# A two-layer encoder on one core: stationary weight tiles read with a step of two values, weight slots at six places modulo 512 bytes

## What is computed

```python
x = x + 0.5 * swiglu(rmsnorm(x, norm_ff1[i]), ff1_w_gate[i], ff1_w_up[i], ff1_w_down[i])   # d_ff = 2816
x = x + token_mixer(rmsnorm(x, norm_mix[i]), w_in[i], ...)      # sparse attention + gated linear attention
x = x + 0.5 * swiglu(rmsnorm(x, norm_ff2[i]), ff2_w_gate[i], ff2_w_up[i], ff2_w_down[i])
g = jax.nn.sigmoid(rmsnorm(x, norm_ple[i]) @ ple_w_gate[i])
x = x + g * (p[i] @ ple_w_proj[i])
```

## Time and profile before

| what | value |
|---|---|
| runs | 1181.10 and 1181.36 us, median 1181.23 us |
| span of the profiled execution, first to last instruction | 1179.5 us |
| PE busy | 1168.9 us (99%), 10534 matmuls |
| PEld busy | 1144.7 us (97%) |
| DVE busy | 814.0 us (69%) |
| ACT busy | 593.7 us (50%) |
| granted TensorE clock, mean | 0.997 of full speed |
| moved by DMA | 218.87 MB, mean 186 GB/s |

### The profile page before, as it was taken

One profiled execution on the slowest core, in us unless ns is written; L12 is line 12 of the kernel. 1 busy time (PEld: TensorE's weight loads), 2 busy tenths in 40 slices (PEclk: granted clock), 3 DMA queues, 4 the chain that ended last, 5 costly groups with the idle time before them and its releaser, 6 DMA issues.

```text
span 1179.5 us, 24037 instructions
## 1 busy us (share of the span) xinstructions
PE 1168.9 (99%) x10534; PEld 1144.7 (97%) x10534; DVE 814.0 (69%) x939; ACT 593.7 (50%) x669; POOL 122.8 (10%) x136
## 2 busy tenths in 40 slices
PE   9999999999999999999999999999999999999997
PEld 9999999999999999999999999999899999999996
DVE  5866555688978766655786665558798777666455
ACT  5544445555745544444554444447367455444443
POOL 2000001011512000001210000100133020000011
PEclk9999999999999999999999999999999999999998
DMA  7655555545445555555555555554635365555541
GB/s 288 235 203 188 193 201 177 184 156 202 145 149 207 190 188 206 183 204 187 179 202 194 194 199 184 197 203 139 214 140 169 118 235 203 184 204 186 186 172 36
DMA packets 33384, 218.87 MB, mean 186 GB/s; under 512 B 5184, under 2 KB 6016, under 8 KB 7296
## 3 DMA queue, kind: packets, MB, share of 16 engines
q1 hardware_dynamic: 33280, 217.34, 53.2%
HBM read 216.15 MB, written 1.05 MB: 184 GB/s over the span
## 4 chain that ended last, share of the span: by engine, by line
PE 98%; DVE 1%; DMA 1%; ACT 0%; issue 0%; POOL 0%; SPq 0%; POOLq 0%; DVEq 0%
PE psum L385 31%; PE psum L387 31%; PE psum L386 31%; PE psum L665 1%; PE psum L644 1%; DMA x_all<-in_x 1%; PE psum L517 0%; PE psum L578 0%; PE psum L628 0%; PE psum L699 0%; PE psum L424 0%; PE psum L710 0%; PE psum L613 0%; DVE gates L1671 0%; PE psum L733 0%
## 5 line engine op out<-in xcount | busy, mean ns | idle before, releaser
L1222 DVE TENSOR_TENSOR w_lo<-raw,w_hi 128x2048 fp32r<-128x2048 f32 x200 | 457.9, 2293 | 213.5 <-ACT w_hi L856 213.4
L856 ACT ACTIVATE w_hi<-raw 128x2048 fp32r<-128x2048 f32 x201 | 385.2, 1917 | 366.6 <-PE psum L387 360.8
L385 PE MATMUL psum<-hA_hi,w_hi 128*128 128x256 f32 x1360 | 377.9, 278 | 0.0
L386 PE MATMUL psum<-hA_hi,w_lo 128*128 128x256 f32 x1360 | 375.7, 276 | 0.0
L387 PE MATMUL psum<-hA_lo,w_hi 128*128 128x256 f32 x1360 | 375.7, 276 | 0.0
L385 PEld LDWEIGHTS psum<-hA_hi,w_hi 128*128 128x128 f32 x1360 | 255.4, 188 | 2.7 <-issue 2.7
L386 PEld LDWEIGHTS psum<-hA_hi,w_lo 128*128 128x128 f32 x1360 | 255.4, 188 | 0.0
L387 PEld LDWEIGHTS psum<-hA_lo,w_hi 128*128 128x128 f32 x1360 | 255.3, 188 | 0.0
L385 PE MATMUL psum<-hB_hi,w_hi 128*128 128x256 f32 x832 | 230.3, 277 | 1.1 <-DVE w_lo L1654 1.1
L386 PE MATMUL psum<-hB_hi,w_lo 128*128 128x256 f32 x832 | 229.7, 276 | 0.0
L387 PE MATMUL psum<-hB_lo,w_hi 128*128 128x256 f32 x832 | 229.7, 276 | 0.0
(11 more groups left out here) (182 smaller groups left out, 1226.0 us busy)
## 6 DMA issues: line engine op xcount, KB each, us to landing
raw<-in_weights SPq DMA_DIRECT2D x203, 1024.0 KB, 4.9
raw<-in_weights SPq DMA_DIRECT2D x2, 512.0 KB, 6.2
out<-gates SPq DMA_DIRECT2D x3, 256.0 KB, 2.2
x_all<-in_x SPq DMA_DIRECT2D x1, 520.0 KB, 3.9
x_all<-in_x SPq DMA_DIRECT2D x1, 512.0 KB, 6.2
relu<-in_p SPq DMA_DIRECT2D x2, 256.0 KB, 5.0
consts<-in_consts SPq DMA_DIRECT2D x1, 384.0 KB, 5.7
out<-gates SPq DMA_DIRECT2D x2, 128.0 KB, 2.3
```

The costliest lines, as they stand in the source:

```text
L385: pe.matmul(o, lh, rh, start=start, stop=False)
L386: pe.matmul(o, ll, rh, start=False, stop=False)
L856: act.activation(w_hi[:, s, :], raw[:, s, :], ACT.Copy).then_inc(hi_ready[s], 1)
L1222: dve.tensor_tensor(w_lo[:, s, :], raw[:, s, :], w_hi[:, s, :].bitcast(F32), ALU.subtract).then_inc(lo_ready[s], 1)
```

## The change

The host alternates the columns of the two output tiles in each block of 256 (`in_turn` in `weight_chunks`, for the chunks of 8 x 256 columns): column 2j is column j of the first tile, 2j + 1 that of the second. The kernel reads a tile back with a step of two values (`in_turn(s)`, then `wh[:, k, c, :]`), so that the 128 values of a stationary tile lie over 1024 bytes where they lay over 512. Chunks of the other kinds are as before.

`w_hi` and `w_lo` become three tiles each, with gaps of 128 bytes: modulo 512, and from the same origin, `w_hi` is at 0, 128 and 256 and `w_lo` at 64, 192 and 320. `hA` and `small` stay at 192. The six small tiles move into the gaps; they leave the place ahead of `hB` and `hid`, and as `BEFORE_HB` is not changed, `hB` and `hid` come to 320. No instruction is added or taken away, on any engine, and no wait.

```diff
-LO_PLACE = 128
+LO_PLACE = 64
+SLOT_STEP = 128
...
-        w_hi = sb("w_hi", [P, SLOTS, 2048], F32R)
-        sb("before_w_lo", [P, LO_PLACE // 4])
-        w_lo = sb("w_lo", [P, SLOTS, 2048], F32R)
-        sb("before_hA", [P, (MOVING_PLACE - LO_PLACE) % 512 // 4])
+        w_hi, w_lo, between = [], [], []
+        for s in range(SLOTS):
+            w_hi.append(sb(f"w_hi{s}", [P, 2048], F32R))
+            between += [sb(f"between{s}{i}", [P, SLOT_STEP // 8]) for i in range(2)]
+        mean, rstd, r_eighth, r_less, r_half, gbias = (t[:, 0:2] for t in between)
+        sb("before_w_lo", [P, (LO_PLACE - SLOTS * SLOT_STEP) % 512 // 4])
+        for s in range(SLOTS):
+            w_lo.append(sb(f"w_lo{s}", [P, 2048], F32R))
+            sb(f"after_w_lo{s}", [P, SLOT_STEP // 4])
+        sb("before_hA", [P, (MOVING_PLACE - LO_PLACE - SLOTS * SLOT_STEP) % 512 // 4])
...
+            def in_turn(s):
+
+                return [w[s][:, :].rearrange("p (k i c) -> p k c i", k=8, c=2) for w in (w_hi, w_lo)]
+
             def by_columns(s, o, h, columns=(0, 1)):
-                wh, wl = (w[:, s, :].rearrange("p (k n) -> p k n", n=256) for w in (w_hi, w_lo))
+                wh, wl = in_turn(s)
                 for c in columns:
                     for k in range(8):
-                        mm = three(o[:, c * T:(c + 1) * T], wh[:, k, c * P:(c + 1) * P], wl[:, k, c * P:(c + 1) * P],
+                        mm = three(o[:, c * T:(c + 1) * T], wh[:, k, c, :], wl[:, k, c, :],
                                    h[0][:, k, :], h[1][:, k, :], k == 0, k == 7)
...
-                            mm = three(bank[DOWN_BANKS[m] + i][:, 0:T], wh[:, u, i * P:(i + 1) * P], wl[:, u, i * P:(i + 1) * P],
+                            mm = three(bank[DOWN_BANKS[m] + i][:, 0:T], wh[:, u, i, :], wl[:, u, i, :],
                                        hid[0][:, k, :], hid[1][:, k, :], k == 0, k == 21)
...
-                act.activation(w_hi[:, s, :], raw[:, s, :], ACT.Copy).then_inc(hi_ready[s], 1)
+                act.activation(w_hi[s][:, :], raw[:, s, :], ACT.Copy).then_inc(hi_ready[s], 1)
...
-                dve.tensor_tensor(w_lo[:, s, :], raw[:, s, :], w_hi[:, s, :].bitcast(F32), ALU.subtract).then_inc(lo_ready[s], 1)
+                dve.tensor_tensor(w_lo[s][:, :], raw[:, s, :], w_hi[s][:, :].bitcast(F32), ALU.subtract).then_inc(lo_ready[s], 1)
...
+    def in_turn(tiles):
+        return tiles.reshape(*tiles.shape[:-1], 2, P).swapaxes(-1, -2).reshape(tiles.shape)
+
+    def pairs(m, c0):
+        return in_turn(columns(m, c0, 256))
```

More of the change, by code:

```diff
@@ L397, in pairs @@
             def pairs(s, first, h, c, ks):
-                wh, wl = (w[:, s, :].rearrange("p (k n) -> p k n", n=256) for w in (w_hi, w_lo))
+                wh, wl = in_turn(s)
                 for k in ks:
-                    mm = three(bank[first + c][:, 0:T], wh[:, k, c * P:(c + 1) * P], wl[:, k, c * P:(c + 1) * P],
+                    mm = three(bank[first + c][:, 0:T], wh[:, k, c, :], wl[:, k, c, :],
                                h[0][:, k, :], h[1][:, k, :], k == 0, k == 7)
@@ L409, in by_tokens @@
             def by_tokens(s, o, h, ks, first, last, ahead=None):
-                wh, wl = (w[:, s, :].rearrange("p (k n) -> p k n", n=512) for w in (w_hi, w_lo))
+                wh, wl = (w[s][:, :].rearrange("p (k n) -> p k n", n=512) for w in (w_hi, w_lo))
                 for i, k in enumerate(ks):
@@ L480, in ffn @@
                     s = operands(L, off + DOWN + c)
-                    wh, wl = (w[:, s, :].rearrange("p (u n) -> p u n", n=256) for w in (w_hi, w_lo))
+                    wh, wl = in_turn(s)
                     for u in range(8):
@@ L534, in mix @@
                 wait_free(pe, L, "small")
-                wh, wl = (w[:, s, 0:1024].rearrange("p (k n) -> p k n", n=P) for w in (w_hi, w_lo))
+                wh, wl = (w[s][:, 0:1024].rearrange("p (k n) -> p k n", n=P) for w in (w_hi, w_lo))
                 for k in range(8):
@@ L797, in embed @@
                 pe.wait_ge(p_lo, L + 1)
-                wh, wl = (w[:, s, :].rearrange("p (k n) -> p k n", n=1024) for w in (w_hi, w_lo))
+                wh, wl = (w[s][:, :].rearrange("p (k n) -> p k n", n=1024) for w in (w_hi, w_lo))
                 for m in range(8):
@@ L886, in split_pieces @@
                 for i in range(4):
-                    act.activation(w_hi[:, s, piece(i)], raw[:, s, piece(i)], ACT.Copy).then_inc(piece_hi if i < 3 else hi_ready[s], 1)
+                    act.activation(w_hi[s][:, piece(i)], raw[:, s, piece(i)], ACT.Copy).then_inc(piece_hi if i < 3 else hi_ready[s], 1)
             def take_rb(L, k, b):
@@ L1112, in _ @@
                 for m in (2 * i, 2 * i + 1):
-                    act.activation(w_hi[:, 0, piece(m)], raw[:, 0, piece(m)], ACT.Copy).then_inc(piece_hi if m < 3 else hi_ready[0], 1)
+                    act.activation(w_hi[0][:, piece(m)], raw[:, 0, piece(m)], ACT.Copy).then_inc(piece_hi if m < 3 else hi_ready[0], 1)
             squares(0, 0, 0)
@@ L1116, in _ @@
             for i in range(4):
-                act.activation(w_hi[:, 1, piece(i)], raw[:, 1, piece(i)], ACT.Copy).then_inc(next_hi if i < 3 else hi_ready[1], 1)
+                act.activation(w_hi[1][:, piece(i)], raw[:, 1, piece(i)], ACT.Copy).then_inc(next_hi if i < 3 else hi_ready[1], 1)
                 if i == 1:
@@ L1653, in _ @@
                         dve.wait_ge(hi_ready[0], 1)
[L1654 removed]
+                    dve.tensor_tensor(w_lo[0][:, piece(m)], raw[:, 0, piece(m)], w_hi[0][:, piece(m)].bitcast(F32), ALU.subtract
                                       ).then_inc(piece_lo if m < 3 else lo_ready[0], 1)
@@ L1688, in weight_chunks, with columns @@
 def weight_chunks(w, L):
-    def columns(m, c0, n=256):
+    def in_turn(tiles):
+        return tiles.reshape(*tiles.shape[:-1], 2, P).swapaxes(-1, -2).reshape(tiles.shape)
+    def pairs(m, c0):
+        return in_turn(columns(m, c0, 256))
+    def columns(m, c0, n):
         return m.reshape(8, P, -1)[:, :, c0:c0 + n].transpose(1, 0, 2)
@@ L1700, in ffn @@
         for g in range(N_FF):
-            out += [columns(gate, 256 * g), columns(up, 256 * g)]
-        units = down.reshape(22, P, 4, 256).transpose(2, 0, 1, 3).reshape(88, P, 256)
+            out += [pairs(gate, 256 * g), pairs(up, 256 * g)]
+        units = in_turn(down.reshape(22, P, 4, 256).transpose(2, 0, 1, 3).reshape(88, P, 256))
         return out + [units[8 * c:8 * c + 8].transpose(1, 0, 2) for c in range(N_FF)]
@@ L1710, in weight_chunks @@
     for c, n in [("iq", 2), ("gq", 1), ("gk", 1), ("aq", 2), ("ak", 2)]:
-        mix += [columns(w_in, COL[c] + 256 * i) for i in range(n)]
+        mix += [pairs(w_in, COL[c] + 256 * i) for i in range(n)]
     for c in ("gv", "gr"):
         mix += [rows(w_in, 4 * i, 512, COL[c]) for i in range(2)]
-    mix += [columns(w_in, COL["mga"] + 256 * i) for i in range(8)]
+    mix += [pairs(w_in, COL["mga"] + 256 * i) for i in range(8)]
     for name in ("w_branch_a", "w_branch_b"):
         mix += [rows(w[name][L], 0, 512, 512 * i) for i in range(2)]
-    mix += [columns(w["w_out"][L], 256 * i) for i in range(4)]
-    ple = [rows(w["ple_w_proj"][L], 0, 1024)] + [columns(w["ple_w_gate"][L], 256 * i) for i in range(4)]
+    mix += [pairs(w["w_out"][L], 256 * i) for i in range(4)]
+    ple = [rows(w["ple_w_proj"][L], 0, 1024)] + [pairs(w["ple_w_gate"][L], 256 * i) for i in range(4)]
     return [c.reshape(P, 2048) for c in ffn("ff1") + mix + ffn("ff2") + ple]
```

10 lines of the change are left out of this document (2 added, 8 removed).

## The result

The changed kernel takes 1236.6 us (1236.3 to 1236.9) against 1181.23: 1.047 times the time before, 95% interval 1.044 to 1.050. The prediction was 1166.5 us with a range of 1140 to 1205, so the change is slower where a small gain was forecast, and the time lies outside the range. (One count in the kernel's description ahead of the prediction is wrong: there are 102 chunks a layer and 204 in all, not 105 and 210. The 90 chunks a layer that the prediction counts with, and the 8640 matmuls, are right.)

The account below looks back on a forecast made before the run. PE's matmul pace was taken as the bound, with the load replacing the moving side. Span 1179.5 - 14.7 = 1164.8 us, all other terms 0, plus 1.7 gave 1166.5 us; range 1140 to 1205.

Parts of the forecast that it names:

- What bounds the kernel: PE, 98% of the chain: time is matmul count times pace, 8640 at 113.3 ns, 979 us of the 1179.5 us span.
- The two streams disturb one another by an amount that their offset sets: PE's moving columns and weight loads: same-shape matmuls follow at 118 ns after a break, then at 113.3.
- Gone is the overtaking: Stationary reads with a step of two pass 1024 bytes like the moving side, so neither stream overtakes; 8640 loads, -14.7 us.
- I take 111.6: Pace forecast for the 8640 step-two loads, from the row of 20 loads of ones: 8640 x (113.3 - 111.6) = -14.7 us.
- a load with a step is slower: Rival: the stepped load itself costs more, 2129 us at half speed, 1263 with a tenth more; chance 0.11.
- The trace has each nearly alone: Rows taken as each stream's floor: transposes at 109 ns for the moving side, ones at 111.6 ns for full loads.
- the rival with a floor of 109: Rival: undisturbed loads follow at less than 109 ns, so the moving side sets 109; 1144 us, chance 0.20.
- Six places, 0 to 6 us: New slot places: 960 `w_lo` loads meet moving tiles at the same place; 6 us at 118 ns, 0 taken.
- Chunks left as they were: Unstepped chunks read from other places: 288 matmuls of 512 columns -3.7 to +3.7 us, 528 others -0.9 to +2.5; 0 taken.
- Splits, DMA, small tiles: ACT and DVE splits at new offsets, SP's same 1 MB transfers and six moved small tiles: all covered or unchanged, 0.
- the rival that the ports are independent: Rival: the streams share nothing, 113.3 ns is the sequencers' handover and no layout changes it; 1181 us, chance 0.16.

Follow-up runs that it names:

- the last study: Kernel before, ahead of its first chunk: step 1 to 4 loads under 16 moving columns, 24-matmul runs between, step-2 loads under float32; 111.7, 117.7, 173.3 to 174.7, 233.3 ns.
- the scans: Kernel before, matmuls on constants at many stationary places ahead of its first chunk: step 1 116.7 to 120.4 ns, step 2 118.3 to 122.3; hi/lo pairs 113.3 to 124.5, 117.8 to 122.3.
- the first study: Kernel before, 256-column matmuls at 32 places for steps 1 and 2, 8 for step 4, then loads under 16 columns; 116.7 to 120.4, 118.3 to 122.3, 233.3 to 235.6 ns.

## Why the prediction was wrong

*What bounds the kernel: right.* PE's pace is the time before and after; 8640 matmuls and one nanosecond for 8.6 us held in each run. No wait came in.

*The two streams disturb one another by an amount that their offset sets: right.* One offset changed by 64 bytes moves the kernel from 113.3 to 118.2 ns and by 43 us.

*"Gone is the overtaking": wrong as the cause.* Streams at one speed still disturb each other when the moving side is F32R at full rate (118.3 to 122.3 ns by place at step 2), and streams at two speeds don't when it is float32 at half (117.7 at all places, as the load alone). The earlier trace rows could not tell these apart: the ones have equal speed and half the moving rate at once, and I read the first out of a row that shows the second just as well.

*"I take 111.6" for a load with a step: the step that failed in size and sign.* The load sets most of the pace, as forecast, but at step 2 it takes 117.7 ns by itself. That is above the 113.3 that the kernel had, so nothing that the layout does beside it could have gained. The rival "a load with a step is slower" named the mechanism and the point from which it decides, 116.0; it had 0.11, with no row for it or against it, since the only rows with a step were moving ones. The Trainium skill, "Advanced Engine Details and Errata", SBUF Cachelines, says that a 16-byte line needs at least two hits to hide the memory's latency. The measurement decides against reading that as a step that is free: at step 2 two values of each line are used, and the load takes 6.0 ns more than 111.7.

*"The trace has each nearly alone": half right.* The transposes of the earlier trace rows are not the moving stream alone. Each has a full load of its own in PEld's timeline of the kernel before, from the first of eight to the next load (342.11 - 341.24) / 8 = 109 ns:

```profile
341.24 0.90 PEld L733 LDWEIGHTS psum<-consts,iqT 128*128 128x128 f32 x8
342.11 0.19 PEld L385 LDWEIGHTS psum<-small_hi,w_hi 128*128 128x128 f32 x1
```

So a short run of loads can go at 109 ns; of the rival with a floor of 109 nothing came, as runs of 16 and more ended at 111.7 even with 16 moving columns beside them.

*Six places, 0 to 6 us: wrong.* I looked for tiles at the same place modulo 512. No tile at the same place is needed: `w_lo` moved by 64 bytes alone gives 118 ns and 43 us, as much as all six places. In the changed kernel the places add nothing that can be seen: 55 us with them, 56 without. That the kernels at 113.3 have `w_lo` 128 bytes from `w_hi` and both 64, modulo 128, from the moving tiles is what the runs show; which of these distances counts stays open.

*Chunks left as they were: the bounds were right.* The contiguous ones of 256 columns go at 118.2, so 528 x 4.9 = +2.6 us, the upper end; those of 512 columns took 0.5 us more.

*Splits, DMA, small tiles: right, 0.*

The sum with measured terms: 8640 x (117.7 - 113.3) = 38 us for the load, 8640 x (119.6 - 117.7) = 16 us that the streams still take from each other, 3 us for the chunks left as they were: 57, against 55.0 measured on the spans. The step alone costs 56 us and the places alone 41, and both together 55 and not 97. Why they don't add is not shown: the load alone (117.7 ns) and the places alone (118.0) both lie below the 119.6 of the two together, so it is not simply that the slower one decides.

Of the rival that the ports are independent, with its 1181 us, the runs leave nothing at full moving rate: `LO_PLACE` alone moved the time by 3.7%. The Trainium skill, "SBUF — State Buffer", Who interferes with whom, calls PE's two read ports independent and has PE wait for nobody; here the pace of its two streams hangs on their places. What the disturbance is inside the memory stays open. So does why the same contiguous run settles at 113.3 in one try and at 117.8 in another: in the last study the run of 24 at one place, at a granted clock of 1.00, ended at 113.3 seven times and at 117.7 or 117.8 five times. A single try of 24 or 36 therefore doesn't tell what a place allows at step 1; the whole kernels do, with thousands of matmuls each. No place at step 1 went below 113.3, so no version that beats the kernel before came out of the scans.

## What to carry to other kernels

A weight load is priced on its own: find in the trace a row with full loads and little moving, and before a stationary tile is read with a step, ask whether the load has room, because where the pace of matmuls stands 1.7 ns above the load's floor, a load 5% longer is already the loss. A comparison row that differs in two things from the state it stands for (here speed and rate) prices neither. And where a layout was found by trying offsets, change one offset at a time, and name every distance that it changes: 64 bytes in one of them were worth 3.7%.

## What was not expected of the hardware

- The load's price by step at the granted clock of 1.00: 111.7, 117.7, 174 and 233.3 ns for 128 values at steps 1 to 4, 239.9 at step 8. The values stand in 32, 64, 96, 128 and 128 groups of four; 117.7 / 64, 174 / 96 and 233.3 / 128 all are 1.8 ns a group. At that price the 32 groups of step 1 would take 58 ns, well under the 111.7 that a load takes anyway; so step 2 is the first at which the groups decide, and only just.
- At a granted clock of 0.50 (the level of 1.2 GHz) the step of two costs nothing. In the first study, 48 step-2 loads and 48 step-4 loads ran at that level, as the busy times of these stretches show (us, PE, PEld, DVE, ACT, POOL, PEclk, DMA share, GB/s), and PEld's timeline has their starts:

```profile
261.00:270.00 9.00, 9.00 (x44) 9.00 (x44) 0.00 (x0) 0.00 (x0) 0.00 (x0) 0.50 0.01 2
272.00:281.00 9.00, 9.00 (x40) 9.00 (x40) 0.00 (x0) 0.00 (x0) 0.00 (x0) 0.50 0.00 0
```

```profile
259.83 10.36 PEld L853 LDWEIGHTS psum<-hA_hi,w_hi 128*128 128x128 f32 x48
270.08 0.54 PEld L829 LDWEIGHTS psum<-ones_r 128*128 128x128 f32 x2
270.50 11.30 PEld L856 LDWEIGHTS psum<-hA_hi,w_hi 128*128 128x128 f32 x48
281.71 0.31 PEld L387 LDWEIGHTS psum<-hB_hi,w_hi 128*128 128x128 f32 x1
```

Step 2 takes 10.25 / 48 = 214 ns, which is what step 1 came to in the same run (213 ns over its last 24 loads, at the same clock), and step 4 takes 11.21 / 48 = 234, the same as at full clock: the price of a group of four doesn't follow the array's clock.

- The disturbance of the two streams repeats after 256 bytes of distance at both steps (116.7 to 120.4 and 118.3 to 122.3 ns by place), and is absent when the moving side reads float32 at half the byte rate (111.7 ns at all 32 places at step 1, 117.7 at all eight at step 2).
